# Two heads of the first tile moved from the expert phase into the front of a decoder-step kernel

## The chip, the cores and the metric

The kernel runs on one core of one Trainium2 chip. The metric is the device time of one execution in microseconds (us), the median of several runs. The profile is of one further execution, with its own time.

## What is computed

One layer of a hybrid decoder on 1024 prompt tokens and 32 sample tokens (8 sequences of 4), all in float32, width 1024. The part that matters here:

```python
h = h + concat(pooling_mixer, conv_module) @ w_out
# PEER product-key experts on x = rmsnorm(h) * g_ffn, blocks of 128 tokens
q = (x @ w_q).reshape(tokens, 8, 2, 128)            # 8 heads, 2 halves
s = einsum('thpc,hpkc->thpk', q, sub_keys)          # 128 keys for each half
sv, si = top_k(s, 16)
cand = sv[:, :, 0, :, None] + sv[:, :, 1, None, :]  # 256 candidates
top_s, top_j = top_k(cand, 16)
eidx = take(si0 * 128 + si1, top_j); gate = softmax(top_s)
u, v = u_tab[eidx], v_tab[eidx]                     # 16384 x 1024 each
coef = gate * gelu(sum(x * u)); h = h + sum(coef * v)
```

Before it stands an input projection with the two mixers, behind it a gated embedding and a final norm. For every token and head 16 rows of 4 KB are gathered from u_tab and 16 from v_tab.

## The kernel before

The kernel is one program with an instruction stream written out for each engine. It has two phases, `front` and `experts`. A phase ends for all engines together: an engine enters the second when all have ended the first.

`front` treats the first four prompt tiles (512 tokens) and the 32 samples: norm, input projection, mixers, layer norm of the convolution, and the output projection. Its last loop goes over two spans of columns (`th` 0: 256 tokens, `th` 1: 288) and eight pieces of the output (`n`). PE makes one product of four matmuls into one of four PSUM results (line 590; the same result is used again four products later, behind `added`). DVE adds it to `hT` (line 733) and adds the squares of the product before to `total` (line 724). ACT squares the piece (line 419) and writes it times the gain `g_ffn` into `xg_a` (lines 422, 424), the input of the queries. SP loads the two first pieces of `w_q` (`wq`, a ring of two, 1 MB each) in the front already; POOL has nothing to do at its end.

`experts` goes over 66 blocks: 64 of one prompt tile and one head (128 tokens by 16 picks), and two of samples. Queries and scores are made in units: the units 0 and 1 (`ALONE`) are heads 0 and 1 for tile 0 alone, the next ones are half a head for the tiles together. `query(s)` (line 1373) and `scores(s)` (line 1384) are PE's, ACT copies the query and scales the scores by `rstd` (lines 1102, 1112), and DVE makes `pick(s)` (lines 1687 to 1697, the best 16 of 128 in two rounds of 8) and `rank_tile` (lines 1703 to 1726, the best 16 of 256, their table indices `eidx` and the shifted scores). POOL issues a gather for each pick (line 1066), one of u and one of v by turns, v 20 picks behind u. The u rows go to a ring of 8, the v rows to a ring of 7. DVE makes the dot product of a u row with the normed tokens `xn` (line 1772), ACT a diagonal matrix of the coefficients (line 1188), and PE multiplies it by the v row and sums in `acc` (line 1671). Later blocks also hold the mixers of the other four tiles, step by step, and the embedding.

At the start of `experts`, SP first issues the broadcast of `g_ffn`, two tiles of x, and then the next pieces of `wq`, each when a query unit has freed its place. PE makes query 0, the means of squares for four tiles, scores 0, query 1, scores 1, turns tile 0, then units 2 to 5. DVE picks and ranks head 0, then head 1, makes `xn`, and begins with the dots. POOL's first gather waits for the first rank (`ranked`).

Of the kernel before, what the change touches and what calls it, by code (L numbers as in the profile page):

```python
# [128 lines left out]
AHEAD_OF_NORM = 5  # L129
WQ_RING = 2  # L130
# [7 lines left out]
def front(nc, io, M):  # L138

    with Phase(nc, "fr") as ph:  # L140
# [33 lines left out]
        part = xT  # L174
        recent = bass.AP(tensor=ufull_s[:, :, :].tensor, offset=0, ap=((DEC_B * (CONV_PRE + DEC_S), P), (CONV_PRE + DEC_S, DEC_B), (1, DEC_S), (1, TAPS)))
# [14 lines left out]
        keys_turned, keys_out = ph.sem("keys_turned"), ph.sem("keys_out")  # L190
# [24 lines left out]
        def gate_count(c):  # L215

            return c + 2

        @block.sync
        def _(sp):  # L220
# [89 lines left out]
        def _(act):  # L310
# [74 lines left out]
            for r in range(4):  # L385
                act.wait_ge(keys_turned, r + 1)
                nc.scalar.copy(flat(M.keysT[:, 4 * r:4 * r + 4, :]), extra[:, r % 2, :]).then_inc(keys_out, 1)
# [24 lines left out]
            nc.scalar.activation(std[:, n_all + 1:n_all + 2], M.eps[:, :], ACT.Sqrt)  # L412
            for th, cols in enumerate(SPANS):
                for n in range(DC):
                    act.wait_ge(added, DC * th + n + 1)
# [3 lines left out]
                    nc.scalar.activation(osq[n % 2][:, cols], M.hT[:, n, cols], ACT.Square).then_inc(squared, 1)  # L419
                    gain = M.vec[:, VEC["g_ffn"] + n:VEC["g_ffn"] + n + 1]  # L420
                    stop = min(cols.stop, SA)
                    nc.scalar.activation(M.xg_a[:, n, cols.start:stop], M.hT[:, n, cols.start:stop], ACT.Copy, scale=gain)
# [4 lines left out]
        def _(pe):  # L427
# [89 lines left out]
            for r in range(4):  # L517
                pe.wait_ge(keys_in, 32)
                if r >= 2:

                    pe.wait_ge(keys_out, r - 1)
                for k in range(4):
                    last = nc.tensor.transpose(extra[:, r % 2, k * P:(k + 1) * P], keys[:, 4 * r + k, :], M.ident[:, :])
                last.then_inc(keys_turned, 1)
# [10 lines left out]
            pe.wait_ge(keys_out, 4)  # L535
# [39 lines left out]
            for n in range(AHEAD_OF_NORM + 1, DC):  # L575
                pool_half(n)
            for th, cols in enumerate(SPANS):
                for n in range(DC):
                    if n == 0:
# [14 lines left out]
        def _(dve):  # L594
# [130 lines left out]

            for th, cols in enumerate(SPANS):
                for n in range(DC):
                    m = DC * th + n
                    if th == 0 and n + 2 in range(AHEAD_OF_NORM, DC):
                        add_part(n + 2)  # L730
                    dve.wait_ge(part_added, n + 1)
                    dve.wait_ge(projected, m + 1)
# [15 lines left out]
HEAD_FIRST = 2  # L748
# [113 lines left out]
def experts(nc, io, M):  # L862

    with Phase(nc, "ex") as ph:
# [11 lines left out]
        eidx = [ph.sb(f"eidx{b}", [P, TOPK], U32) for b in range(KEPT)]  # L876
# [1230 lines left out]
```

## Time and profile before

| | |
|---|---|
| median of 3 runs | 3347.69 us (3325.36 to 3354.73) |
| the profiled execution's own time | 3370.43 us |
| its span, first to last instruction | 3368.6 us |
| mean granted TensorE clock | 0.931 of full |
| PE / DVE / ACT / POOL busy | 80% / 67% / 24% / 62% |
| bytes moved by DMA | 1167.87 MB, 347 GB/s over the span |

Busy shares are means over stages that differ. The rows below give start times in us from the span's start. In a timeline row the second number is the time from the group's start to its end, xN the number of instructions, and the bracket the idle time before it with what ended that.

### The profile page before, as it was taken

How to read it: one execution, taken by the hardware profiler on the slowest of the kernel's cores; microseconds unless marked ns; L12 is line 12 of the kernel's file. 1: busy time of each engine (PE TensorE's matmuls, PEld its weight loads, DVE VectorE, ACT ScalarE, POOL GpSimd, SP SyncE). 2: the span in 40 equal slices, each digit the busy share in tenths (PEclk: the TensorE clock that was granted, in tenths of full speed). 3: DMA queues.
4: the chain of work that ended last, by engine and by line, in shares of the span. 5: the costliest groups of instructions: out<-in, count | busy, mean ns of one | idle time of the engine just before them, and what ended most of it. 6: DMA issues, size and time to landing. Idle time of an engine off the chain costs nothing.

```text
span 3368.6 us, 24895 instructions
## 1 busy us (share of the span) xinstructions
PE 2698.3 (80%) x6723; PEld 1222.9 (36%) x6723; DVE 2268.0 (67%) x5244; ACT 815.5 (24%) x1946; POOL 2097.5 (62%) x2169
## 2 busy tenths in 40 slices
PE   8989888888978767677688887789878888678867
PEld 7754433333333323333344442233323333223322
DVE  8867668897875766767767565656566668555545
ACT  2332322223131211111112222222222222112212
POOL 2135666676766667566566666666666667666664
PEclk9999998999999988888899989999999999899998
DMA  5269999999999999899899999999999999999996
GB/s 142 70 236 354 359 367 346 381 387 377 377 363 350 396 368 370 331 354 346 326 367 373 360 361 410 386 367 376 378 365 365 376 376 371 357 360 367 374 370 211
DMA packets 363167, 1167.87 MB, mean 347 GB/s; under 512 B 35401, under 2 KB 88217, under 8 KB 363029
## 3 DMA queue, kind: packets, MB, share of 16 engines
q0 software_dynamic: 304128, 1107.43, 86.5%
q1 hardware_dynamic: 58368, 58.02, 5.3%
q8 instruction: 57, 0.93, 0.1%
q10 hardware_dynamic: 533, 0.83, 0.1%
q14 instruction: 81, 0.66, 0.1%
HBM read 1160.98 MB, written 5.15 MB: 346 GB/s over the span
## 4 chain that ended last, share of the span: by engine, by line
PE 22%; DVE 19%; POOL 15%; issue 13%; another core or an unknown queue 13%; DMA 10%; ACT 2%; DVEq 0%; POOLq 0%; ACTq 0%
PE ex_acc L1671 14%; DVE ex_u_row L1772 8%; POOL ex_v_row L1066 8%; POOL ex_u_row L1066 7%; DMA ex_u_row<-in_u_tab_dram,ex_eidx 5%; DMA ex_v_row<-in_v_tab_dram,ex_eidx 4%; PE ex_q L1373 3%; PE ex_turn L1429 2%; DVE m_mix L1865 1%; PE ex_q L1429 1%; DVE m_hT L1790 1%; DVE ex_lists L1697 1%; DVE ex_lists L1690 1%; DVE ex_same L1691 1%
## 5 line engine op out<-in xcount | busy, mean ns | idle before, releaser
L1671 PE MATMUL ex_acc<-ex_v_row,ex_diag 128*128 128x512 f32 x3840 | 1919.3, 639 | 556.3 <-DMA ex_v_row<-in_v_tab_dram,ex_eidx 290.5
L1772 DVE CUSTOM_DVE_ANT_0 ex_u_row<-ex_u_row,ex_xn 128x1024 f32<-128x1024 f32 x1056 | 1256.2, 1217 | 482.0 <-DMA ex_u_row<-in_u_tab_dram,ex_eidx 358.8
L1066 POOL DMA_INDIRECT ex_v_row<-in_v_tab_dram,ex_eidx x1024 | 995.2, 972 | 598.1 <-issue 271.8
L1671 PEld LDWEIGHTS ex_acc<-ex_v_row,ex_diag 128*128 128x128 f32 x3840 | 726.7, 201 | 1651.8 <-issue 1503.5
L1066 POOL DMA_INDIRECT ex_u_row<-in_u_tab_dram,ex_eidx x1024 | 996.0, 973 | 527.4 <-issue 285.2
L1188 ACT ACTIVATE ex_diag<-m_ident,ex_coef 128x128 f32<-128x128 f32 x948 | 318.7, 393 | 737.4 <-issue 326.6
L1373 PE MATMUL ex_q<-m_mix,m_wq 128*128 128x384 f32 (+3 forms) x832 | 238.4, 441 | 2.4 <-PEq L95 1.9
L1373 PEld LDWEIGHTS ex_q<-m_mix,m_wq 128*128 128x128 f32 x832 | 143.1, 193 | 104.0 <-issue 66.9
L1102 ACT COPY ex_qT<-ex_q 128x384 f32<-128x384 f32 (+3 forms) x50 | 22.0, 440 | 475.5 <-remote 313.4
L1384 PE MATMUL ex_s<-m_keysT,ex_qT 128*128 128x128 f32 x288 | 54.1, 328 | 79.3 <-ACT ex_qT L1102 63.4
L1790 DVE SCALAR_TENSOR_TENSOR m_hT<-ex_v_row,ex_coef,m_hT 128x1024 f32<-128x1024 f32 x76 | 97.4, 1282 | 0.0
L1763 DVE SCALAR_TENSOR_TENSOR ex_coef<-ex_expo,ex_norm,ex_hact 128x16 f32<-128x16 f32 x64 | 15.2, 238 | 117.9 <-issue 70.6
L1510 PE MATMUL ex_turn<-m_hT,m_wq 128*128 128x512 f32 x192 | 89.0, 607 | 5.4 <-ACT m_mix L1214 5.4
L1772 DVE DVE_READ_ACCUMULATOR2_ANT ex_hdot<- 128x1 f32 x1056 | 87.7, 83 | 0.4 <-issue 0.4
L1384 PEld LDWEIGHTS ex_s<-m_keysT,ex_qT 128*128 128x128 f32 x288 | 44.8, 219 | 111.5 <-ACT ex_qT L1102 75.7
L1112 ACT ACTIVATE ex_score<-ex_s,ex_rstd 128x128 f32<-128x128 f32 (+1 forms) x144 | 42.3, 363 | 174.1 <-PE ex_s L1384 87.0
L1277 ACT ACT_TABLE_LOAD x65 | 83.4, 1283 | 1.1
L1865 DVE SCALAR_TENSOR_TENSOR m_mix<-m_mix,m_taps 128x512 f32<-128x512 f32 x109 | 82.3, 755 | 1.3 <-issue 0.9
L1118 ACT ACT_TABLE_LOAD x63 | 80.8, 1283 | 1.1
L1694 DVE MAX8 ex_lists<-ex_same 128x8 f32<-128x128 f32 (+1 forms) x144 | 32.6, 281 | 63.1 <-remote 60.5
L1277 ACT ACTIVATE ex_hact<-ex_hdot 128x16 f32<-128x16 f32 x66 | 14.2, 215 | 233.5 <-DVE ex_hdot L1772 159.2
L1429 PE MATMUL ex_turn<-m_mix,m_wq 128*128 128x512 f32 x128 | 61.3, 624 | 6.2 <-ACT m_wq L1142 6.2
(371 smaller groups left out, 2037.6 us busy)
## 6 DMA issues: line engine op xcount, KB each, us to landing
m_wq<-in_w_q_dram SPq DMA_DIRECT2D x18, 1024.0 KB
ex_u_row<-in_u_tab_dram,ex_eidx POOLq DMA_INDIRECT x1024
ex_v_row<-in_v_tab_dram,ex_eidx POOLq DMA_INDIRECT x1024
fr_w<-in_w_in_dram SPq DMA_DIRECT2D x12, 512.0 KB, 4.3
m_wq<-in_w_in_dram SPq DMA_DIRECT2D x6, 1024.0 KB
m_wq<-in_w_out_dram SPq DMA_DIRECT2D x4, 1024.0 KB
m_mix<-in_w_ple_gate_dram SPq DMA_DIRECT2D x8, 512.0 KB
out_y_prompt_dram<-m_wq SPq DMA_DIRECT2D x7, 512.0 KB
```

Of the source, the lines that this page charges most:

```text
L1066: pool.indirect_dma_start(out=row[:, :], out_offset=None, in_=table, in_offset=bass.IndirectOffsetOnAxis(ap=picks(b)[:, k:k + 1], axis=0)) ...
L1118: nc.scalar.activation(expo[r % KEPT][:, :], shift[r % 2][:, :], ACT.Exp, accum_out=norm[r % KEPT][:, :]).then_inc(exped, 1)
L1188: nc.scalar.activation(diag[:, n % DIAGS, 0:rows(t)], pattern[:, :], ACT.Copy, scale=coef[b % 2][:, k:k + 1]).then_inc(diaged, 1)
L1277: nc.scalar.activation(hact[b % 2][:, :], hdot[b % 2][:, :], ACT.Gelu_apprx_tanh).then_inc(gelued, 1)
L1373: last = nc.tensor.matmul(q_ps[:, out:out + cols], weights(load, c), xg[:, c, at:at + cols], start=(c == 0), stop=(c == DC - 1))
L1384: last = nc.tensor.matmul(s_ps[0:rows(t), j * P:(j + 1) * P], qT[:, s % 2, j * P:j * P + rows(t)], keysT[:, half, :], start=True, stop=True)
L1429: last = nc.tensor.matmul(gate_out[:, :], x2T[:, c, :], w_gate[:, c, cols], start=(c == 0), stop=(c == DC - 1))
L1510: last = nc.tensor.matmul(late_bank[n % 2], weights(late_load(n), c), late_h[:, c, :], start=(c == 0), stop=(c == DC - 1))
L1671: last = nc.tensor.matmul(acc[0:rows(t), half, :], diag[:, tensor_sums(n) % DIAGS, 0:rows(t)], row[:, half * HALF_D:(half + 1) * HALF_D], ...
L1772: nc.vector.tensor_tensor_reduce(out=u_row[n % U_RING][:, :], in0=u_row[n % U_RING][:, :], in1=xn[:, :], scale=1.0, scalar=0.0, op0=ALU.mu ...
L1790: ins = nc.vector.scalar_tensor_tensor(out=tokens, in0=row[:, :].rearrange("p (c e) -> p c e", c=DC), scalar=coef[b % 2][:, k:k + 1], in1= ...
L1865: nc.vector.scalar_tensor_tensor(out=u, in0=src, scalar=tap[:, j:j + 1], in1=u, op0=ALU.mult, op1=ALU.add).then_inc(late_tapped, 1)
```

## The change

The units 0 and 1 leave `experts`. Their work is done in the last loop of `front`, in its second span. PE makes one mean (tile 0) and query 0 ahead of product 1, scores 0 ahead of product 2, query 1 ahead of product 3, scores 1 ahead of product 4. ACT takes the root, the two query copies and the two scaled scores between its squares. DVE makes the reciprocal ahead of add 1, pick 0 ahead of add 2, the rank of head 0 ahead of add 3 and pick 1 ahead of add 5. The query and score use columns of `val` and `gate` that no result uses, and the small tiles lie in `xin`, which is free by then. In the first span ACT now writes the gained tokens ahead of the square. The lists of head 1, the index list and the shifted scores of head 0 get tiles that outlive the front. SP loads the next two pieces of `wq` in the front too, each behind the query that frees its place.

At the start of `experts` the semaphores are counted up for what is done already, DVE begins with the rank of head 1, and PE begins with the four means (now into `s_ps`), turns tile 0 and goes on with unit 2. The reciprocals of the four tiles come behind the rank.

```diff
+HEAD_FIRST = 2
+QUERY_BEFORE = (1, 3)
+SCORE_BEFORE = (2, 4)
...
# front, SP
+            for n in range(WQ_RING):
+                sp.wait_ge(projected, query_count(n))
+                sp.dma_start(M.wq[:, n], wq_cols[:, :, 2 * (n + WQ_RING) * P:2 * (n + WQ_RING + 1) * P]).then_inc(M.wq_in[n], 16)
...
# front, ACT
+            def first_root():
+                act.wait_ge(meaned, len(SPANS) + 1)
+                nc.scalar.activation(first_std, small[:, 0, 0:1], ACT.Sqrt, bias=M.eps[:, 0:1]).then_inc(rooted, 1)
+
+            def first_query_out(h):
+                act.wait_ge(projected, query_count(h))
+                if h > 0:
+
+                    act.wait_ge(keyed, 4 + h)
+                nc.scalar.copy(flat(first_qT), first_q).then_inc(part_out, 1)
+
+            def first_scores_out(h):
+                act.wait_ge(keyed, 4 + h + 1)
+                act.wait_ge(inverted, n_all + 1)
+                nc.scalar.activation(flat(first_score[h]), first_s, ACT.Copy, scale=first_rstd).then_inc(keyed_out, 1)
+
             for th, cols in enumerate(SPANS):
                 for n in range(DC):
+                    if th == 1 and n == 1:
+                        first_root()
+                        first_query_out(0)
+                    if th == 1 and n == 2:
+                        first_scores_out(0)
+                    if th == 1 and n == 3:
+                        first_query_out(1)
+                    if th == 1 and n == 4:
+                        first_scores_out(1)
...
# front, PE
+            def first_mean():
+                pe.wait_ge(totalled, DC + 1)
+                pe.wait_ge(added, DC)
+                nc.tensor.matmul(small[:, 0, 0:1], M.total[:, 0:P], M.mean_d[:, 0:1], start=True, stop=True).then_inc(meaned, 1)
+
+            def first_query(h):
+                pe.wait_ge(squared, n_all + 2 * MC + DC)
+                pe.wait_ge(M.wq_in[h], 16)
...
+                for half in range(2):
+                    for c in range(DC):
+                        last = nc.tensor.matmul(first_q[:, half * P:(half + 1) * P], M.wq[:, h, c, half * P:(half + 1) * P], M.xg_a[:, c, 0:P],
+                                                start=(c == 0), stop=(c == DC - 1))
+                last.then_inc(projected, 1)
...
# front, DVE: first_pick(h) and first_rank_head() have the steps of pick and rank_tile
                     m = DC * th + n
+                    if th == 1 and n == 1:
+                        dve.wait_ge(rooted, n_all + len(SPANS) + 1)
+                        nc.vector.reciprocal(first_rstd, first_std).then_inc(inverted, 1)
+                    if th == 1 and n == 2:
+                        first_pick(0)
+                    if th == 1 and n == 3:
+                        first_rank_head()
+                    if th == 1 and n == 5:
+                        first_pick(1)
...
# experts, SP
-            for pair in range(WQ_RING, LOADS // 2):
+            for pair in range(2 * WQ_RING, LOADS // 2):
...
# experts, PE
-            query(0)
+            pe.sem_inc(q_done, ALONE)
+            pe.sem_inc(scored, ALONE)
             for t in range(A_TILES):
-                last = nc.tensor.matmul(turn[:, 0, t:t + 1], M.total[:, t * P:(t + 1) * P], M.mean_d[:, 0:1], start=True, stop=True)
+                last = nc.tensor.matmul(s_ps[:, t:t + 1], M.total[:, t * P:(t + 1) * P], M.mean_d[:, 0:1], start=True, stop=True)
             last.then_inc(meaned, 1)
-            scores(0)
-            query(1)
-            scores(1)
-            pe.wait_ge(rooted, 1)
             turn_tokens(0)
-            for s in range(2, EARLY):
+            for s in range(ALONE, EARLY):
                 query(s)
+                if s == ALONE:
+                    pe.wait_ge(rooted, 1)
                 scores(s)
...
# experts, DVE
+            dve.sem_inc(picked, ALONE)
+            dve.sem_inc(ranked, 1)
+            dve.sem_inc(shifted, 1)
+            rank_tile(1)
             dve.wait_ge(rooted, 1)
             nc.vector.reciprocal(rstd[:, 0:A_TILES], std[:, 0:A_TILES]).then_inc(inverted, 1)
-            for head in range(HEAD_FIRST):
-                pick(head)
-                dve.wait_ge(picked, head + 1)
-                rank_tile(head)
+            dve.wait_ge(inverted, 1)
```

## Rows read from the trace of the kernel before

**Rows 1.** The page, DMA queues: packets, MB, share of 16 engines

```profile
q0 software_dynamic: 304128, 1107.43, 86.5%
...
q14 instruction: 81, 0.66, 0.1%
```

**Rows 2.** Windows by stage: length, busy time by engine, clock, DMA share, GB/s

```profile
207.50:300.00 92.50, 74.54 (x207) 35.74 (x206) 70.30 (x221) 24.02 (x61) 56.32 (x59) 0.90 0.94 349
300.00:1000.00 700.00, 598.37 (x1393) 260.53 (x1392) 557.16 (x1325) 189.06 (x479) 465.73 (x471) 0.94 0.97 371
1000.00:2000.00 1000.00, 765.07 (x1888) 352.04 (x1888) 676.90 (x1715) 198.30 (x510) 644.28 (x660) 0.90 0.95 357
2000.00:3000.00 1000.00, 792.72 (x1751) 317.90 (x1750) 608.18 (x1311) 254.60 (x563) 667.50 (x696) 0.95 0.98 374
3000.00:3330.00 330.00, 247.83 (x540) 94.16 (x539) 170.74 (x306) 69.30 (x156) 217.40 (x223) 0.93 0.95 357
```

**Rows 3.** Timeline of PE, 150 to 214 us

```profile
175.25 2.10 PE L590 MATMUL fr_val<-fr_mix,fr_wout 128*128 128x288 f32 x8
...
188.84 2.10 PE L590 MATMUL fr_small<-fr_mix,fr_w 128*128 128x288 f32 x8
192.88 3.81 PE L1373 MATMUL ex_q<-m_mix,m_wq 128*128 128x128 f32 x32 [1.94 <-PEq L95]
196.53 0.95 PE L1606 MATMUL ex_turn<-m_mean_d,m_total 128*128 128x1 f32 x8
197.34 0.69 PE L1384 MATMUL ex_s<-m_keysT,ex_qT 128*128 128x128 f32 x4
...
204.07 7.11 PE L1373 MATMUL ex_q<-m_mix,m_wq 128*128 128x512 f32 x16 [0.42 <-DMA m_wq<-in_w_q_dram]
```

**Rows 4.** Timeline of DVE, 150 to 214 us, then 213 to 262 us

```profile
185.23 0.46 DVE L733 TENSOR_TENSOR m_hT<-m_hT,fr_val 128x288 f32<-128x288 f32 x1 [1.12 <-PE fr_val L590]
185.60 0.45 DVE L724 TENSOR_TENSOR m_total<-m_total,fr_odd 128x288 f32<-128x288 f32 x1
...
192.01 0.46 DVE L724 TENSOR_TENSOR m_total<-m_total,fr_odd 128x288 f32<-128x288 f32 x1
...
198.84 0.49 DVE L1687 MAX8 ex_lists<-ex_score 128x8 f32<-128x128 f32 x2 [0.86 <-ACT ex_score L1112]
...
201.71 0.43 DVE L1703 TENSOR_TENSOR ex_cand<-ex_lists 128x256 f32<-128x256 f32 x1
...
207.01 0.17 DVE L1721 SCALAR_TENSOR_TENSOR ex_eidx<-ex_idx 128x16 uint32<-128x16 f32 x1
...
215.52 1.29 DVE L1960 SCALAR_TENSOR_TENSOR ex_xn<-m_hT,ex_rstd,ex_g_ffn 128x1024 f32<-128x1024 f32 x1
```

**Rows 5.** Timeline of ACT, 150 to 214 us

```profile
192.28 0.30 ACT L424 ACTIVATE m_mix<-m_hT,m_vec 128x32 f32<-128x32 f32 x1
```

**Rows 6.** Timeline of POOL, 180 to 420 us

```profile
207.47 1.15 POOL L1066 DMA_INDIRECT ex_u_row<-in_u_tab_dram,ex_eidx  x1 [85.18 <-DVE ex_eidx L1721]
```

**Rows 7.** Timeline of SP, 100 to 330 us

```profile
192.85 0.38 SPq L1024 DMA_DIRECT2D ex_g_ffn<-in_g_ffn_dram  x1
193.27 0.89 SPq L1022 DMA_DIRECT2D ex_lists<-in_x_prompt_dram  x2
```

**Rows 8.** Windows of 2 to 5 us, columns as in rows 2

```profile
206.00:208.00 2.00, 2.00 (x6) 0.81 (x5) 1.90 (x9) 0.31 (x2) 0.53 (x1) 1.00 0.12 38
208.00:210.00 2.00, 2.00 (x6) 0.95 (x5) 1.93 (x13) 0.00 (x0) 1.56 (x2) 1.00 0.27 39
210.00:212.00 2.00, 1.32 (x4) 0.35 (x3) 1.86 (x8) 0.58 (x1) 1.52 (x2) 1.00 0.93 324
...
260.00:265.00 5.00, 5.00 (x19) 2.79 (x18) 4.76 (x15) 0.13 (x2) 3.75 (x4) 1.00 0.60 186
```

**Rows 9.** Waits of ACT, then of DVE, whole span: us in total, times, longest

```profile
ACT ex_qT L1102 <- remote: 313.4, 22, 21.9
...
DVE ex_lists L1694 <- remote: 60.5, 11, 8.0
```

More of the change, by code:

```diff
@@ L217, in gate_count, with output_count, query_count @@
             return c + 2
+        def output_count(th, n):
+            return DC * th + n + 1 + (sum(n >= QUERY_BEFORE[h] for h in range(HEAD_FIRST)) if th == 1 else 0)
+        def query_count(h):
+            return output_count(1, QUERY_BEFORE[h]) - 1
         @block.sync
@@ L385, in _ @@
             for r in range(4):
-                act.wait_ge(keys_turned, r + 1)
-                nc.scalar.copy(flat(M.keysT[:, 4 * r:4 * r + 4, :]), extra[:, r % 2, :]).then_inc(keys_out, 1)
+                act.wait_ge(keyed, r + 1)
+                nc.scalar.copy(flat(M.keysT[:, 4 * r:4 * r + 4, :]), extra[:, r % 2, :]).then_inc(keyed_out, 1)
             for g in range(MC):
@@ L576, in _, with first_scores @@
                 pool_half(n)
+            def first_mean():
[5 more added lines that the diff above has]
+                pe.wait_ge(M.wq_in[h], 16)
+                if h > 0:
+                    pe.wait_ge(part_out, DC + h)
+                for half in range(2):
[3 more added lines that the diff above has]
+                last.then_inc(projected, 1)
+            def first_scores(h):
+                pe.wait_ge(part_out, DC + h + 1)
+                if h > 0:
+                    pe.wait_ge(keyed_out, 4 + h)
+                for half in range(2):
+                    last = nc.tensor.matmul(first_s[:, half * P:(half + 1) * P], first_qT[:, half, :], M.keysT[:, 2 * h + half, :],
+                                            start=True, stop=True)
+                last.then_inc(keyed, 1)
             for th, cols in enumerate(SPANS):
                 for n in range(DC):
+                    if th == 1 and n == QUERY_BEFORE[0]:
+                        first_mean()
+                        first_query(0)
+                    if th == 1 and n == SCORE_BEFORE[0]:
+                        first_scores(0)
+                    if th == 1 and n == QUERY_BEFORE[1]:
+                        first_query(1)
+                    if th == 1 and n == SCORE_BEFORE[1]:
+                        first_scores(1)
                     if n == 0:
@@ L724, in total_squares, with first_pick @@
                 nc.vector.tensor_tensor(M.total[:, cols], M.total[:, cols], osq[m % 2][:, cols], ALU.add).then_inc(totalled, 1)
+            def first_pick(h):
+                values, at = head_lists[h][:, 0], head_lists[h][:, 1].bitcast(U32)
+                dve.wait_ge(keyed_out, 4 + h + 1)
+                for half in range(2):
+                    last = nc.vector.max(values[:, half, 0:8], first_score[h][:, half, :])
+                chain.step(last)
+                for half in range(2):
+                    nc.vector.max_index(at[:, half, 0:8], values[:, half, 0:8], first_score[h][:, half, :])
+                    last = nc.vector.match_replace(first_rest[:, half, :], values[:, half, 0:8], first_score[h][:, half, :], NEG)
+                chain.step(last)
+                for half in range(2):
+                    last = nc.vector.max(values[:, half, 8:16], first_rest[:, half, :])
+                chain.step(last)
+                for half in range(2):
+                    last = nc.vector.max_index(at[:, half, 8:16], values[:, half, 8:16], first_rest[:, half, :])
+                chain.step(last)
@@ L1343, in _ @@
             few_sigmoids(2)
-            nc.scalar.activation(few_moment[:, 3:4], M.eps[0:TS, 0:1], ACT.Sqrt)
+            nc.scalar.activation(few_moment[:, 2:3], M.eps[0:TS, 0:1], ACT.Sqrt)
             act.wait_ge(few_biased, 1)
```

77 lines of the change are left out of this document (59 added, 18 removed).

## The prediction

> **What bounds the kernel now.** I read the queues first. Gathers from the two expert tables (POOL's software queue) are 1107 MB of the kernel's 1168 MB and alone fill 86.5% of the sixteen DMA engines' span [rows 1]. Then the windows by stage: from 300 to 3330 us the DMA engines are 95 to 98% busy at 357 to 374 GB/s, while PE is busy 75 to 85% of the time, DVE 52 to 80% and POOL about two thirds [rows 2]. So behind the first gathers the time is bytes through the DMA engines. 2112 gathers of 0.524 MB have to pass, and an edit that leaves these bytes alone can only change when the stream begins, how full it is kept, and the tail. The reader is to see that DMA share is the one column near 1 in every long stage. The change touches the 192.6 to 300 us stretch and nothing behind it, where the share is already 0.94 [rows 2].
>
> Then the order of work at the seam. PE's last output product starts at 188.84 us [rows 3], DVE's last sum of squares is at 192.01 [rows 4], ACT's last gain ends at 192.58 [rows 5], and 0.3 us later PE has its first instruction of the experts' phase, at 192.88 [rows 3]. POOL's first gather comes at 207.47 [rows 6], right behind the write of the first index list at 207.01 [rows 4]. These 14.9 us between seam and first gather are what the change goes for.
>
> **Part 1, PE in the front.** One query of 32 matmuls takes from 192.88 to 196.53, 3.65 us; four mean matmuls take 0.81, so one is 0.2; the four score matmuls take 0.69 alone, 0.55 with the overlap at their end [rows 3]. Output products of the second span start 1.94 us apart: (188.84 - 175.25) / 7 [rows 3]. The mean added ahead of product 1 needs the sum of square 7, which DVE does only behind the add of product 0: for the product that starts at 183.01 (four steps behind 175.25) that pair ends at 186.05, 3.0 us after the product's start [rows 3, 4]. So the mean can start at 178.3 while product 0 ends at 177.2: a new wait of 1.1 us on PE; behind it on PE are all the other products. PE's front grows by 1.1 + 0.2 + 2 x 3.65 + 2 x 0.55 = 9.7 us, and its last product ends near 200.5.
>
> **Part 2, DVE in the front.** A pick takes from 198.84 to 201.71, 2.9 us; the ranking from 201.71 to 207.18 (the index list's 207.01 + 0.17), 5.5 us [rows 4]; the added reciprocal of one column I take at 0.2, like the shortest DVE row there. Together 2 x 2.9 + 5.5 + 0.2 = 11.5 us. An add and a sum of squares take 0.82 us of the 1.94 us step [rows 4], so DVE has 1.1 us free in each step, far less than it gets. Followed through: the first query ends at 182.2, product 1 at 184.1, the first scores at 184.7; ACT turns to them behind its own square and gains, and the first pick starts near 186.0. Three pieces (2.9 + 5.5 + 2.9), six add and sum pairs (4.9) and the last sum (0.45) then run nearly without a gap, to 202.7; with waits for ACT's squares between them I take 203.9, and ACT's last gain 204.1. Queued behind the picks are the adds of products 2, 3 and 5, for which ACT's squares wait. PE wants a bank back only four products later, and by this count never stands for an add: product 7 wants the add of 3, done at 195.9, and starts at 198.5. DVE, then, not PE, ends the front: 204.1 against 192.6, 11.5 us later. Bounds: 202.7 (no waits) and 206.5 (a further 1.1 us wait for each of ACT's two score copies).
>
> **Part 3, the first gather.** The index list is there when the phase opens, so POOL needs the 0.3 us of the seam and 0.3 us as between 207.18 and 207.47 [rows 4, 6]: 204.1 + 0.6 = 204.7 or 204.8. That is 2.7 us earlier than now; bounds 203.3 and 207.1, so 4.2 to 0.4 us earlier. 14.9 us are taken out behind the seam, 11.5 put in ahead of it, and that is why the large move pays little.
>
> **Part 4, the other queues.** SP issues the two weight pieces (1 MB each) behind query 0 and query 1 in the front, near 182 and 190, where nothing else moves. They landed before 207 so far, ahead of the first gather, in time the DMA engines would mostly have stood: the share is 0.12 in 206 to 208 and 0.27 in 208 to 210 [rows 8]. So moving them out frees almost nothing; they saved only the 0.42 us wait of PE at 204.07 [rows 3]. What was not moved matters more: the gain vector's broadcast and two x tiles, 0.5 MB each, go out when the phase opens, at 192.85 and 193.27 [rows 7]. Now they were through long before the gathers; after the change they are issued in the same microsecond as the first gather. 1.5 MB at 371 GB/s (the mean of the 300 to 1000 window [rows 2]) is 4.0 us. Some 2.3 us of that fits into the time in which the first row is being set up (gather at 207.47, full rate only from 210 [rows 6, 8]), so rows arrive 0 to 4.0 us later than their issue would allow; I take 1.7. Net of part 3: 1.0 us earlier, between 4.2 earlier and 3.6 later.
>
> By the Trainium skill ("DMA: Bandwidth & Descriptors", section "Queues, rings and completion order") each DMA engine takes turns between the queue rows that have work, packet by packet. By that rule the three loads would halve the first rows' rate rather than hold them all back; the bytes, and so the sum, stay the same.
>
> **Part 5, DVE and PE in the new phase.** DVE starts with the second ranking (5.5), then xn (1.3), so its first dot comes near 211.6; now it follows xn at 215.52 + 1.3 = 216.8 [rows 4]: 5 us earlier. But dots then wait for rows, which are 1 us ahead. PE's units 2 to 5 come later: query 2 starts behind the means and the turn of tile 0 at 206.4, against 204.07 [rows 3]. Their scores are first picked behind sixteen dots, whose rows come no faster than 0.524 MB / 371 GB/s = 1.41 us each, so not before 211.6 + 16 x 1.41 = 234; units 2 and 3, 7.1 us each [rows 3] and some 1.5 for copy and scores, end near 223.6. That cover of 10 us makes the cost nothing; without it it is 2.3 us. A last piece is a hole in the DMA stream: 0.60 busy from 260 to 265 [rows 8], 2 us lost there, when DVE was late with picks and dots. With DVE 5 us ahead it may shrink by these 2 us or stay: I take half, 1 us earlier.
>
> **Sum.** 1.0 + 1.0 = 2 us earlier. On the profiled execution 3370.4 - 2 = 3368.4. Its span is 3368.6 and the rest of it is 1.8. The median of the runs shown is 22.7 us below it, and the gain is not a share of the length, so 3347.7 - 2 = 3345.7.
>
> **Rivals.** (a) The head start counts in full: the loads hide wholly in the set-up time, DVE's 5 us fill both the hole at 260 and the ones behind it. For it: POOL waits on DVE's dots in that stretch. Against it: a ring of eight rows, which DVE empties faster than they come. It gives 4.2 + 5 = 9 us less, 3338.5. (b) Slower, by stalls of the engines in straight code. ACT waits 313.4 us in 22 times ahead of its query copies for something that the profile calls remote, up to 21.9 us, and DVE does so between two steps of one pick, up to 8.0 us [rows 9]. The instruction queue moves its own packets on the same DMA engines [rows 1]. A saturated stream now begins earlier, with loads on top. If one more such wait of 21.9 falls on ACT ahead of the first gate or diagonal, the rings' fifteen rows cover 15 x 0.524 MB / 371 GB/s = 21 us less what already waits; with half of them in hand, 11 us are lost: 3347.7 - 2 + 11 = 3356.7. It decides if the first weighted sum starts over 10 us later against the first gather than now. The Trainium skill ("Runtime: NRT & Kernel Launch", section "Instruction fetch mechanics") says that the fetch across a block is mostly hidden; by that rule this rival would cost nothing, but it has no account of the remote waits seen here. (c) The change doesn't start the gathers earlier: DVE's front stretches to 206.5 or more, the loads then delay the rows by up to 4: 3347.7 + 3.6 = 3351.
>
> **How the numbers follow.** Chances: forecast 0.5, (a) 0.17, (b) 0.15, (c) 0.13, and 0.05 for something that no row shows. All four lie within 11 us, a third of 1%. The three runs before lie from 3325.4 to 3354.7, so 1% (33 us) is about what a measurement can tell, and this spread, not the mechanism, makes the range: 3320 (the lowest run less 5) to 3361 (the highest and half of (b)). Faster by over 1%: 0.06, from (a) with a lucky spread and a part of the unknown; slower by over 1%: 0.06, from (b) twice; within 1%: 0.88.
>
> **What would show it.** The phase opens near 204, the first gather is near 204.8, the first dot near 211.6; DVE has no gap over 1 us between the first front pick and the last sum; PE's products keep their 1.94 us step except at the queries; the DMA share from 300 on stays 0.95 to 0.98. I am wrong if PE waits for adds, if the front ends behind 206.5, or if the time moves by more than 10 us, which would need the DMA's rate in the long stages to have changed.

## The result, and the profile after

The changed kernel takes 3354.15 us (median of 21 runs, 3345.12 to 3379.32) against 3346.15 us (21 runs, 3313.93 to 3364.1) on the same chip: ratio 1.0042, 95% interval 1.0023 to 1.006. That is 8 us slower by the medians and 14 us by the ratio. The profiled execution took 3359.54 us with a span of 3357.7; it is shorter than the profiled one of before (3368.6), so the ends of two single profiles can't show the loss. The gathers, in order, show where the stream falls behind:

```
start of POOL's n-th gather, us      n=0    n=8    n=20   n=28   n=32   n=48   n=60   n=100  n=200  n=300
before                              207.5  219.2  235.1  250.4  260.2  285.2  302.2  367.0  524.6  670.8
after                               203.9  215.3  230.2  247.3  266.5  289.2  313.5  377.6  534.1  680.8
after minus before                   -3.5   -3.9   -5.0   -3.1   +6.2   +4.0  +11.3  +10.6   +9.5   +9.9
```

The stream starts 3.5 us early, keeps that for 28 gathers, and is 10 us late from the 60th on. Behind the 400th the difference wanders between 10.5 us early and 14.1 us late; the last gather starts 10.2 us earlier than before. So these two profiles show the lag at the start, and not what is left of it at the end.

The seam first: the changed kernel's timelines of PE, DVE, ACT, SP and POOL, columns as in [rows 3 to 7].

```profile
197.43 2.10 PE L684 MATMUL fr_small<-fr_mix,fr_w 128*128 128x288 f32 x8
203.48 1.02 PE L1747 MATMUL ex_s<-m_mean_d,m_total 128*128 128x1 f32 x8 [3.95 <-PEq L95]
...
205.57 8.42 PE L1513 MATMUL ex_q<-m_mix,m_wq 128*128 128x512 f32 x16
```

```profile
202.31 0.46 DVE L818 TENSOR_TENSOR m_total<-m_total,fr_odd 128x288 f32<-128x288 f32 x1 [0.48 <-ACT fr_odd L478]
...
211.53 1.22 DVE L1913 CUSTOM_DVE_ANT_0 ex_u_row<-ex_u_row,ex_xn 128x1024 f32<-128x1024 f32 x1 [1.11 <-DMA ex_u_row<-in_u_tab_dram,m_first_idx]
```

```profile
202.58 0.31 ACT L482 ACTIVATE m_mix<-m_hT,m_vec 128x32 f32<-128x32 f32 x1
```

```profile
203.15 0.35 SPq L1165 DMA_DIRECT2D ex_g_ffn<-in_g_ffn_dram  x1
203.55 0.90 SPq L1163 DMA_DIRECT2D ex_lists<-in_x_prompt_dram  x2
```

```profile
203.94 1.15 POOL L1207 DMA_INDIRECT ex_u_row<-in_u_tab_dram,m_first_idx  x1 [82.54 <-DVEq L2088]
...
266.47 0.94 POOL L1207 DMA_INDIRECT ex_u_row<-in_u_tab_dram,ex_eidx  x1 [14.47 <-DVE ex_hdot L1913]
```

The front ends at 202.9, 10.3 us later than before (192.58 [rows 5]), and the first gather comes 3.5 us earlier. But the last line is a gather that waited 14.47 us for a free row. The windows show what that did to the stream (columns as in [rows 8], the long ones as in [rows 2]).

```profile
206.00:208.00 2.00, 2.00 (x3) 0.68 (x2) 1.89 (x5) 1.98 (x2) 1.70 (x2) 0.50 0.99 338
208.00:210.00 2.00, 2.00 (x6) 0.91 (x5) 1.91 (x5) 0.44 (x3) 1.39 (x3) 0.91 1.01 412
...
255.00:260.00 5.00, 4.37 (x16) 2.52 (x17) 0.39 (x3) 3.34 (x8) 0.00 (x0) 1.00 0.84 266
260.00:265.00 5.00, 5.00 (x13) 2.28 (x12) 4.86 (x33) 2.04 (x6) 0.00 (x0) 1.00 0.02 8
265.00:270.00 5.00, 5.00 (x19) 2.63 (x18) 4.86 (x13) 0.26 (x1) 2.81 (x3) 1.00 0.34 98
...
207.50:300.00 92.50, 67.95 (x189) 32.95 (x189) 63.77 (x188) 17.53 (x50) 48.16 (x51) 0.89 0.88 328
300.00:1000.00 700.00, 601.78 (x1404) 259.19 (x1404) 555.34 (x1326) 199.41 (x494) 466.75 (x472) 0.95 0.98 371
1000.00:2000.00 1000.00, 760.77 (x1896) 349.88 (x1895) 678.40 (x1717) 195.12 (x503) 646.88 (x663) 0.90 0.95 358
2000.00:3000.00 1000.00, 795.26 (x1752) 322.03 (x1751) 605.43 (x1303) 254.06 (x563) 662.48 (x695) 0.95 0.98 375
```

From 206 to 210 the DMA engines are full where they stood at 0.12 and 0.27 [rows 8]. From 260 to 265, where they were 0.60 busy, they now stand still: 8 GB/s. The stretch to 300 falls from 0.94 to 0.88; the long stages are as before [rows 2].

Why POOL waits is read backwards. POOL's rows come free with DVE's dots. DVE's timeline shows what stood ahead of them: the coefficients of block 0, which waited for ACT's Gelu. ACT's timeline shows why the Gelu was late, after first and then before:

```profile
259.62 0.23 DVE L1904 SCALAR_TENSOR_TENSOR ex_coef<-ex_expo,ex_norm,ex_hact 128x16 f32<-128x16 f32 x1 [11.34 <-ACT ex_hact L1417]
```

```profile
236.86 1.14 ACT L1253 ACTIVATE ex_score<-ex_s,ex_rstd 128x128 f32<-128x128 f32 x4 [12.78 <-remote]
...
244.04 0.59 ACT L1243 COPY ex_qT<-ex_q 128x512 f32<-128x512 f32 x1 [5.85 <-remote]
246.79 1.14 ACT L1253 ACTIVATE ex_score<-ex_s,ex_rstd 128x128 f32<-128x128 f32 x4 [2.16 <-PE ex_s L1524]
255.00 0.59 ACT L1243 COPY ex_qT<-ex_q 128x512 f32<-128x512 f32 x1 [7.06 <-PE ex_q L1513]
256.83 1.14 ACT L1253 ACTIVATE ex_score<-ex_s,ex_rstd 128x128 f32<-128x128 f32 x4 [1.25 <-PE ex_s L1524]
...
259.29 0.21 ACT L1417 ACTIVATE ex_hact<-ex_hdot 128x16 f32<-128x16 f32 x1
```

```profile
237.08 1.14 ACT L1112 ACTIVATE ex_score<-ex_s,ex_rstd 128x128 f32<-128x128 f32 x4 [7.88 <-remote]
247.86 0.58 ACT L1102 COPY ex_qT<-ex_q 128x512 f32<-128x512 f32 x1 [9.63 <-remote]
250.61 1.14 ACT L1112 ACTIVATE ex_score<-ex_s,ex_rstd 128x128 f32<-128x128 f32 x4 [2.17 <-PE ex_s L1384]
...
253.06 0.22 ACT L1277 ACTIVATE ex_hact<-ex_hdot 128x16 f32<-128x16 f32 x1
```

In both kernels ACT stands in a wait that the profile calls remote until about 237. Before, it held the scores of unit 4, and only unit 5 was left; after, it held the scores of unit 3, and units 4 and 5 were left. PE had begun its units 1.5 us later and run the first query slower (8.42 us instead of 7.11 [rows 3], at a granted clock of 0.50 in 206 to 208). But the wait is also there earlier: PE ended unit 3's scores at 225.3 and ACT did not take them, while before ACT still copied unit 4's query at 228.61. The experiments tell how far PE's delay counts. ACT's order puts the units 4 and 5 ahead of block 0's Gelu in both kernels. The Gelu slips from 253.06 to 259.29, though its last dot ended at 234, not 239. DVE waits 11.34 us for it with the next dots queued behind. The gather that comes at 266.47 waits for one of these dots.

### The profile page after: what moved, and what is told of

The parts are those of the page before. It is cut to its first block, busy times and chain, and to the rows that moved or that the text cites. A ratio compares the mean times of both kernels' runs of the same rounds, so it can differ in the third digit from the quotient of the medians.

```text
span 3357.7 us, 24911 instructions
## 1 busy us (share of the span) xinstructions
PE 2688.2 (80%) x6725; PEld 1217.1 (36%) x6725; DVE 2268.1 (68%) x5245; ACT 815.4 (24%) x1945; POOL 2090.1 (62%) x2169
## 4 chain that ended last, share of the span: by engine, by line
DVE 20%; PE 18%; POOL 17%; issue 14%; another core or an unknown queue 12%; DMA 11%; ACT 2%; DVEq 0%; POOLq 0%; ACTq 0%
PE ex_acc L1810 12%; POOL ex_u_row L1207 8%; POOL ex_v_row L1207 8%; DVE ex_u_row L1913 8%; DMA ex_v_row<-in_v_tab_dram,ex_eidx 5%; DMA ex_u_row<-in_u_tab_dram,ex_eidx 4%; PE ex_q L1513 3%; DVE m_mix L2006 1%; DVE m_hT L1931 1%; DMA ex_u_row<-in_u_tab_dram,m_first_idx 1%; PE ex_turn L1569 1%; PE ex_q L1569 1%; ACT ex_diag L1329 1%; DVE ex_same L1855 1%
## 5 line engine op out<-in xcount | busy, mean ns | idle before, releaser
L1207 POOL DMA_INDIRECT ex_v_row<-in_v_tab_dram,ex_eidx x768 | 741.8, 966 | 455.4 <-issue 200.6
L1207 POOL DMA_INDIRECT ex_u_row<-in_u_tab_dram,ex_eidx x768 | 745.3, 970 | 348.8 <-issue 217.9
L1207 POOL DMA_INDIRECT ex_u_row<-in_u_tab_dram,m_first_idx x256 | 249.7, 976 | 185.3 <-DVEq L2088 82.5
L1207 POOL DMA_INDIRECT ex_v_row<-in_v_tab_dram,m_first_idx x256 | 250.1, 977 | 143.2 <-issue 69.4
L1513 PE MATMUL ex_q<-m_mix,m_wq 128*128 128x384 f32 (+2 forms) x768 | 231.6, 455 | 0.0
L1513 PEld LDWEIGHTS ex_q<-m_mix,m_wq 128*128 128x128 f32 x768 | 135.9, 194 | 101.4 <-issue 64.3
L1243 ACT COPY ex_qT<-ex_q 128x384 f32<-128x384 f32 (+2 forms) x48 | 21.3, 443 | 407.9 <-remote 253.4
```

The lines of the kernel that those rows point to most:

```text
L1207: pool.indirect_dma_start(out=row[:, :], out_offset=None, in_=table, in_offset=bass.IndirectOffsetOnAxis(ap=picks(b)[:, k:k + 1], axis=0)) ...
L1513: last = nc.tensor.matmul(q_ps[:, out:out + cols], weights(load, c), xg[:, c, at:at + cols], start=(c == 0), stop=(c == DC - 1))
```

## The experiments

The order of work in block 0 after the change, on ACT: copy and scores of units 2, 3, 4, 5, then the Gelu, then the diagonals. Theory G says that the Gelu's place behind the units costs the hole. The rivals are the loads beside the first gathers, PE's later start, and its clock. The expectations name more theories by letters: Q is the earlier and wider form of G (the coefficients of block 0 are queued on ACT and PE behind late units), L the loads beside the first gathers, R a cost in the later stages, N a mere scatter of the runs, D the depth of the queued gathers as the reason of ACT's waits. All ratios are to the kernel before on the same chip. Gathers are compared with those of the first profile of before, unless said otherwise; a second profile of that same kernel has gather 0 1.7, gather 32 4.6 and gather 100 1.2 us earlier.

**The loads.** The two x tiles are issued behind the next pair of weight pieces (near 224) instead of in the opening:

```diff
-            load_x(0)
-            load_x(1)
             for pair in range(2 * WQ_RING, LOADS // 2):
                 ...
+                if pair == 2 * WQ_RING:
+                    load_x(0)
+                    load_x(1)
```

> The changed kernel, with the loads of the two x tiles (1 MB) issued behind the next weight piece, near 224, and no longer beside the first gathers. Theory L: rows come up to 2.7 us earlier at the start, the hole near 260 shrinks, ratio 1.001 or less. Theory Q: the rows of the first dots come earlier but the Gelu still waits for unit 5; the ratio stays within 0.1% of 1.004.

Ratio 1.0035 (1.0003 to 1.0068). The first dot comes at 211.22 with no wait for its row, but DVE waits 11.9 us for the Gelu, gather 32 is 6.8 and gather 100 13.1 us later than before. The loads are not the cause.

**PE later in the kernel before.** Sixteen products of the identity ahead of unit 2:

```diff
+            pe.wait_ge(q_out, 2)
+            for j in range(16):
+                nc.tensor.matmul(q_ps[...], M.ident[:, :], M.ident[:, :], start=True, stop=True)
             for s in range(2, EARLY):
```

> The kernel before with 16 added products of the identity (128 columns, some 3.7 us) on PE ahead of unit 2, their result unused: nothing of the front, the gathers' start or the loads changes, only PE's units come later. Theory Q: this alone brings the changed kernel's picture, one unit fewer done when ACT's long wait comes, DVE waiting about 10 us for the first Gelu and a hole in the DMA stream; ratio 1.002 to 1.005. Theories L and R, and a delay that is hidden: 0.999 to 1.001.

Ratio 1.0026 (1.0001 to 1.0052). Unit 2's query starts at 207.21, 3.1 us later than before, twice the delay that the change brings. ACT's unexplained waits hold unit 4's copy to 240.46 (14.31 us), the Gelu comes at 255.97 (before: 253.06), DVE waits 5.1 us (10 were expected), gather 32 is 2.9 and gather 100 8.2 us late. Twice the delay of PE gives half of the lag at gather 32: a delay of PE alone can do damage, but doesn't account for all of it.

**PE kept running at the seam.** The same sixteen products at the end of the changed kernel's front, so that PE does not idle 3.95 us ahead of the phase:

> The changed kernel with 16 products of the identity (3.7 us, unused) on PE at the end of the front, where it stood idle from 199.5 to 203.5 and its granted clock then fell to half in 206 to 208. If idle PE and its clock make the units late: query 2 takes 7.1 us instead of 8.4, unit 3 is ready 1.4 us earlier, gather 100 comes 1 to 5 us earlier, ratio 1.001 to 1.004. If not: gather 100 at 376 to 379 and the ratio within 0.1% of 1.004; above 1.005 if the added products themselves delay the phase.

```profile
204.66 7.03 PE L1516 MATMUL ex_q<-m_mix,m_wq 128*128 128x512 f32 x16
```

The first query is back at 7.03 us and starts a microsecond earlier (PE's timeline), 0.6 us later than before. The hole stays: an unexplained wait of 18.43 us on ACT ends at 243.51, the Gelu comes at 259.1, DVE waits 11.6 us, gather 32 is 6.0 us late; ratio 1.0064 (1.0032 to 1.0097). Gather 100 is 8.0 us late and not 10.6, which is within the gain that the expectation asked for; two profiles of the kernel before differ by 1.2 us at that gather and by 4.6 at gather 32, so 2.6 us may be scatter. So the clock does not make the hole, nor does PE's late start have to: with PE only 0.6 us late the hole is whole. Which of ACT's steps the wait hits decides, and why it hits an earlier one in the changed kernel, where the gathers start earlier too, was not tested.

**The Gelu ahead of unit 5 on ACT.**

```diff
+                if s == 4:
+                    act.wait_ge(dotted, TOPK)
+                    nc.scalar.activation(hact[0][:, :], hdot[0][:, :], ACT.Gelu_apprx_tanh).then_inc(gelued, 1)
```

> The changed kernel; only on ACT the Gelu of block 0 moves ahead of unit 5's query and scores, PE's order stays. If the queue on ACT alone makes the loss: DVE's wait for the Gelu falls from 11.3 us to under 3, gather 32 at 256 instead of 266.5, gather 100 at 367 to 370, ratio 1.000 to 1.002. If PE's lateness makes it (units 5 and 6 stand ahead of the first weighted sum on PE, which starts at 263.5): gather 32 comes earlier but POOL then waits for a v row to be summed, gather 100 stays at 375 to 378, ratio 1.003 to 1.005.

ACT's timeline and two windows of this kernel:

```profile
242.61 1.14 ACT L1253 ACTIVATE ex_score<-ex_s,ex_rstd 128x128 f32<-128x128 f32 x4 [16.95 <-remote]
...
250.14 0.21 ACT L1417 ACTIVATE ex_hact<-ex_hdot 128x16 f32<-128x16 f32 x1
255.59 0.58 ACT L1243 COPY ex_qT<-ex_q 128x512 f32<-128x512 f32 x1 [5.24 <-PE ex_q L1517]
```

```profile
260.00:265.00 5.00, 5.00 (x13) 2.13 (x12) 4.79 (x13) 0.70 (x2) 0.74 (x1) 1.00 0.95 341
...
207.50:300.00 92.50, 74.20 (x208) 36.29 (x206) 64.52 (x189) 21.58 (x55) 53.63 (x57) 0.92 0.96 360
```

The unexplained wait is there, longer than in the changed kernel (16.95 us against 12.78), and PE is as late (unit 5's copy at 255.59, first weighted sum at 264.10). Still the hole at 260 to 265 is gone (0.95 against 0.02), gather 32 comes at 257.3, 2.9 us ahead of before, and gather 100 is 2.1 us late instead of 10.6. Only the Gelu's place was changed: that order is what lets the wait through to the stream. Ratio 1.0004 (0.9965 to 1.0043), where the kernel with the added products took 1.0064 on the same chip. A second series:

> The same kernel as a_gelu_first, for a narrower interval: 1.0004 with 0.9965 to 1.0043 did not part it from the changed kernel's 1.0042. If ACT's queue ahead of block 0's Gelu makes the loss (theory G): 0.999 to 1.002 again, gather 32 near 257, gather 100 near 369. If the first value was luck: 1.003 to 1.006.

1.0017 (0.9992 to 1.0042), gather 32 4.3 us early, gather 100 5.5 us late. Ahead of unit 4 instead (`if s == 3`):

> The changed kernel with the Gelu of block 0 one unit earlier still, behind unit 3's scores and ahead of unit 4's query on ACT. It waits for the sixteenth dot (near 235), so unit 4's query copy and PE's query 5 come about 10 us later. Theory G alone: as a_gelu_first or up to 2 us better, 0.998 to 1.002. If PE's units now become the bound as they did in two_later: gather 32 near 255, gather 100 at 372 or later, ratio over 1.003.

The Gelu ran at 240.37; 1.0011 (0.9977 to 1.0044), gather 32 5.6 us early, gather 100 5.5 us late, as above. What is left is a smaller loss behind gather 32, where POOL waits for PE's weighted sums (15.7 us in 257 to 310, in the first of the three).

**The same place tried on the kernel before.** The Gelu ahead of unit 5:

> The kernel before with the Gelu of block 0 ahead of unit 5's query and scores on ACT. There DVE waited only 2.0 us for it, so theory G gives a gain of 2 us at most: ratio 0.998 to 1.000, gather 32 at 257 to 260, gather 100 at 363 to 367. A kernel-wide effect of the moved Gelu (table loads, order) that has nothing to do with the wait would give this kernel the same 0.4% that it gives the changed one: 0.996.

0.9981 (0.9954 to 1.0008): gather 32 2.3 us early, gather 100 4.9 us early, but the interval holds 1. And the reverse, the Gelu held until unit 6's query is done (`act.wait_ge(q_done, EARLY + 1)` ahead of it):

> The kernel before with one added wait: ACT makes the Gelu of block 0 only when the query of unit 6 is done on PE (258.9 in the trace of before), as if one more unit stood ahead of it. Nothing else is touched, and the gathers start at 207.5. Theory G: DVE waits 7 to 9 us for the Gelu instead of 2.0, POOL waits for the dots behind it, the DMA share falls under 0.4 somewhere in 255 to 270, gather 100 at 372 to 377, ratio 1.002 to 1.004. If a hole there is made up for later: 1.000.

Waits of DVE and windows of this kernel:

```profile
DVE ex_coef L1765 <- ACT ex_hact L1279: 10.6, 1, 10.6
```

```profile
260.00:265.00 5.00, 4.75 (x11) 2.20 (x12) 4.86 (x32) 1.84 (x6) 0.00 (x0) 1.00 0.00 0
```

With nothing of the change in it, one late Gelu (259.19) makes the same hole, and gather 32 is 6.1 us late as in the changed kernel (6.2), gather 100 6.4 late and not the 10 that the changed kernel is. The ratio, 1.0022 (0.9993 to 1.0052), has an interval that holds 1.

**Fewer units ahead of block 0.** Units 4 and 5 moved into block 0's sums, four units there instead of two, in the changed kernel and in the one before:

```diff
-EARLY = 6
+EARLY = 4
...
+                    if b == 0 and k in (0, 5, 10, 13):
+                        query(EARLY + (0, 5, 10, 13).index(k))
```

> The changed kernel, but only units 2 and 3 are made ahead of block 0; units 4 and 5 move into it (units 4 to 7 at its picks 0, 5, 10 and 13), so ACT meets the Gelu of block 0 behind unit 3's scores. Theory Q (the coefficients of block 0 are queued on ACT and PE behind units 2 to 5, and the change makes these units late): ACT's Gelu comes within 3 us of the sixteenth dot (near 240, not 259.3), DVE's wait of 11.3 us ahead of the first coefficients and the hole in the DMA stream near 260 go, gather 60 comes at 303 or earlier instead of 313.5, and the time is 0.2 to 0.6% under the changed kernel's, so 0.998 to 1.002 of the kernel before. Theory L (what costs is the broadcast and the two x tiles beside the first gathers): nothing of that changes, the ratio stays at 1.004. Theory R (the later stages pay, through other tile places or other timing of waits): 1.004 too, with gather 60 early all the same.

> The kernel before with the same order of units. Theory Q: there the Gelu stood at 251.8 behind unit 5 and DVE waited 2.0 us for it, PE's first weighted sum came at 258.7; with the units later both come near 245 to 250, the dip of the DMA share at 260 to 265 shrinks, and the ratio is 0.996 to 1.000. With a_two_later it then gives what the early gather alone is worth: 3 to 4 us. Theories L and R: 1.000, and a_two_later minus this stays at +0.4%.

1.008 (1.0052 to 1.0108) and 1.0081 (1.005 to 1.0111). The hole goes (gather 32 is 5.7 and 4.7 us early), but PE can't carry two more units in block 0: in the first, PE is busy throughout 290 to 340 and the DMA engines are at 0.67.

```profile
290.00:340.00 50.00, 48.56 (x137) 23.34 (x136) 20.29 (x68) 14.71 (x35) 18.57 (x20) 1.00 0.67 224
```

Gather 100 is 19.6 and 18.1 us late. That both kernels lose the same, with first gathers 3.9 us apart, speaks for it that an early first gather is worth nothing where PE sets the pace. Spreading the units over the blocks instead (EARLY = 4, two per block up to block 6, two late products moved with them; units 16 and 17 then read a part of the input that the late mixer has already overwritten, so these two compute other picks there):

> The changed kernel, with units 2 and 3 alone ahead of block 0 and two units in each of the blocks 0 to 6 (before: four ahead and two in each of 0 to 5); one pair of late weights is scaled, and its product made, a few picks later in block 6. What two_later showed: the hole at 250 to 266 goes (gather 32 at 254.6, not 266.5), but four units of 8 us in block 0 put PE behind. Theory Q': early PE work and its order are the bound of the first blocks; with two units in each block PE never has more than 2 x 8 + 16 x 1.7 = 43 us of work in a block whose rows take 32 x 1.41 = 45 us, so the lead of 4 to 6 us at gather 32 stays: gather 100 at 361 to 368 against 367.0 before and 377.6 changed, ratio 0.996 to 1.000. Rival: PE has fallen behind for good in any order, since the same units have to be made before block 6; gather 100 then comes at 375 or later, ratio 1.003 to 1.008.

> The kernel before with the same units in the same blocks. Theory Q': gather 32 near 256 (now 260.2), gather 100 at 363 to 369, ratio 0.998 to 1.001, and 0.001 above a_spread, by the 3.5 us that the gathers start later. Rival: as for a_spread, 1.003 to 1.008.

1.004 (1.0007 to 1.0073) and 1.0019 (0.999 to 1.0048). The start is good (gather 100 is 4.0 us early in the first), and it is lost between gathers 220 and 260, where PE makes the last two of these units: from 6.3 us early to 10.4 late in the first, from 1.9 early to 12.6 late in the second.

**A chip without these waits.** The next four kernels ran on another chip:

> The changed kernel itself, once more, timed beside the two reordered ones so that they can be compared directly. Theory G (the Gelu of block 0 stands in ScalarE's order behind unit 5's copy and scores, VectorE's coefficients wait 11 us for it, and the transfers have a hole at 260 to 265): a ratio of 1.003 to 1.006 to the kernel before, VectorE's wait for the Gelu 10 to 12 us, gather 32 about 6 us and gather 100 about 10 us later than before. Rival N (the first result was a scatter of the runs, as the single profiles scatter by 10 us and more): a ratio of 1.000 to 1.002.

> The changed kernel with block 0's Gelu ahead of unit 5's query copy on ScalarE, beside the changed kernel in the same series. Theory G: 0.002 to 0.004 below the ratio of the changed kernel, that is 1.001 to 1.002, with VectorE's wait for the Gelu 1 to 3 us, gather 32 at 3 to 4 us earlier than before and gather 100 at 2 to 5 us later. Rival N: the same ratio as the changed kernel to 0.001.

> The kernel before with the same reordering on ScalarE, the version that could beat both; its first series gave 0.9981 with an interval that holds 1. Theory G gives it 2 us (the wait of VectorE for the Gelu is 2.0 us before, and gather 32 came 2.3 us earlier): 0.9994, hardly to be told from 1. If the first series is to be taken at its word, 0.998.

> The changed kernel where GpSimd keeps only four gathered rows ahead of the dots during the first 32 gathers, so that fewer transfers stand in the queues at 210 to 240 us. If ScalarE's long unexplained wait (12.78 us, ending at 236.86) comes from the depth of the queued gathers (theory D), it shrinks to under 5 us, the Gelu starts before 255 and VectorE's wait for it is under 5 us; the time is then 1.000 to 1.003. If the depth has nothing to do with it, the wait stays at 8 to 15 us, ends at 237 or later, and the hole stays; the time is 1.004 or more, since the gathers come later too.

The kernel before takes 3077.06 us there, the changed one 3077.3 (ratio 1.0000, 0.9991 to 1.0009), the Gelu ahead of unit 5 3076.92 in the changed kernel (1.0001, 0.9992 to 1.001) and 3076.97 in the one before (0.9998, 0.9989 to 1.0008). Windows and ACT's timeline of the changed kernel there:

```profile
260.00:265.00 5.00, 5.00 (x13) 2.28 (x12) 5.00 (x9) 0.00 (x0) 3.74 (x4) 1.00 0.98 339
...
300.00:1000.00 700.00, 623.44 (x1489) 269.73 (x1488) 581.86 (x1346) 205.87 (x510) 511.68 (x509) 0.98 1.02 402
```

```profile
232.08 0.59 ACT L1243 COPY ex_qT<-ex_q 128x512 f32<-128x512 f32 x1 [5.53 <-PE ex_q L1513]
...
245.07 0.21 ACT L1417 ACTIVATE ex_hact<-ex_hdot 128x16 f32<-128x16 f32 x1
```

No engine shows a remote wait in the whole span. PE is as late at the start as in the first profile (its query takes 8.01 us), yet the Gelu runs at 245.07, DVE waits 3.5 us for it, and the share stays at 0.98. So the hole needs the unexplained wait as well as the order. The loads beside the gathers, the late PE and its clock are all there, and no hole. The first gather at 204.6 and the full queues hold a lead of 2.7 us at the start and 1.7 at gather 300 over the kernel before with its Gelu moved (a profile of the kernel before itself wasn't taken on this chip); at the end it is 1.9 us behind. A gain of 2 us is within what this series can't see.

The kernel with four rows in flight tells nothing on why ACT waits, as no wait was there to shrink; but it prices a hole. POOL waited 28.7 us for dots up to 270 us; it was 20.9 us behind the changed kernel at gather 28, 11.2 at gather 100, 12.4 at gather 300 and 12.7 at the last, and took 3092.66 us, 15.4 more (to the kernel before 1.0055, 1.0039 to 1.007). Between gathers 28 and 60 it gained 9 us back, for there the changed kernel's own stream stood for dots. From then on nothing was regained: what the stream is behind at gather 60 (11.8 us), it is behind at the end.

**Both once more, side by side.**

> The kernel before itself, as a profile beside the changed one on the same chip. The last series ran on a chip whose profiles hold none of ScalarE's long unexplained waits and move 402 to 406 GB/s from 300 us on (371, 358 and 375 in the first profiles); there all kernels but the one with four rows took 3077 us. On such a chip theory G expects: no unexplained wait, the Gelu of block 0 within 3 us of its last dot and unit 5, gather 100 at 351 to 353 us (the reordered one: 351.2), and the ratio of the kernel to itself 1.000. On a chip as in the first series: 3340 to 3370 us, an unexplained wait of ScalarE of 7 to 15 us that ends at 237 to 248, VectorE's wait for the Gelu 2 to 4 us, gather 100 at 364 to 370 us.

> The changed kernel beside it. Theory G: on a chip without the unexplained waits a ratio of 0.999 to 1.001 and gather 100 at 349 to 350 us, 2 us earlier than the kernel before, with a transfer share above 0.9 at 250 to 270; on a chip with them 1.003 to 1.006, VectorE's wait for the Gelu 8 to 12 us, a share under 0.4 somewhere at 255 to 270, gather 100 5 to 12 us later than the kernel before. Rival N (a scatter): no difference on either.

This was a chip of the first kind. The first gathers are at 205.81 and 203.34, so the head start is 2.5 us here. The windows at 260 us, the kernel before first:

```profile
260.00:265.00 5.00, 5.00 (x13) 2.14 (x12) 4.90 (x10) 0.00 (x0) 1.63 (x3) 1.00 0.78 292
```

```profile
260.00:265.00 5.00, 5.00 (x13) 2.28 (x12) 4.90 (x28) 1.17 (x3) 0.00 (x0) 1.00 0.01 2
```

The hole is back, with 13.44 us of unexplained wait on unit 3's scores to 236.87, 11.1 us of DVE for the Gelu, and gather 100 at 379.3 against 365.8. But the times are 3345.66 for the changed kernel and 3344.24 for the kernel before. Each was set against the same 23 further runs of the kernel before (3341.66): 1.0007 (0.9977 to 1.0037) for the changed one, and 1.0006 (0.9976 to 1.0036) for that kernel against itself. The loss of the first series is not seen here, though the hole is; the two intervals share 1.0023 to 1.0037. The spans of the two profiles of one and the same kernel before are 3368.6 and 3318.0 us.

## Why the prediction was wrong

It said 2 us faster; it was slower, by 8 us of the medians and 14 by the ratio. That the time lies inside the range given comes from the spread of the runs, which made the range, and not from the mechanism.

**Parts 1 to 3 held**, within a microsecond or so. PE's last product starts at 197.43 and ends at 199.5 (said: 200.5), with a wait of 0.95 us for the mean (said 1.1). DVE's last sum of squares is at 202.31, ACT's last gain ends at 202.9 (said 204.1, bounds 202.7 to 206.5): DVE ended the front, and it stood less for ACT's squares than I allowed. The first gather came 3.5 us earlier, and 2.5 in the second pair of profiles (said 2.7).

**Part 4 held in its sign.** DVE had `xn` ready at 210.42 and waited 1.11 us for the first row, to 211.53; I had allowed 1.7 us for the loads. Moved away, they freed this wait and changed nothing behind it. That 211.53 is so near to the 211.6 of part 5 is luck: that was DVE's own work, counted from a gather at 204.8, without a wait for the row.

**Part 5 failed**, at one sentence: PE's units 2 to 5 come later, and a "cover of 10 us makes the cost nothing". I measured the cover at the place where DVE picks from the units. There it held: DVE picked from unit 2 at 234.02 without a wait, as said (234). But ACT, which has to copy them, is a queue too, and block 0's Gelu stands behind them. Nothing in the sum asked what was queued behind ACT's copies, and my row on the remote waits [rows 9] stood only in a rival. The cover ended at the Gelu: its last dot was ready at 234, it ran at 259.29. That a reordering of this one step takes the hole away with PE as late as ever, and that one late Gelu puts it into the kernel before, is shown. The dip at 260 to 265, which I let shrink by 1 us, deepened: the DMA share there fell from 0.60 to 0.02.

**Rival (b)** was nearest: a stall of ACT in straight code, 3356.7 us. Its waits were the ones that mattered, but they need not be more or longer than before (ACT's copies wait 253.4 us for "remote" in 21 times, 313.4 in 22 before [rows 9]), and its point of decision, the first weighted sum over 10 us later against the first gather, came to 8.3: 263.50 - 203.94 = 59.6 against 258.74 - 207.47 = 51.3. The place was the Gelu, not the first diagonal. Rival (c)'s 3351 us is as near to the measured time, but its condition failed: the front ended at 202.9, not at 206.5 or later. In the changed kernel's trace no packet of the instruction queues starts between 215.4 and 249.0 us, a stretch that holds both waits of ACT, to 236.86 and to 244.04. So these waits don't test the rule of the Trainium skill ("Runtime: NRT & Kernel Launch", section "Instruction fetch mechanics") that instruction fetch is mostly hidden.

**Whether 10 us are regained** depends on the slack behind them. On the faster chip, with a share of 1.02, they are not: the kernel with four rows was 11.8 us behind at gather 60 and 12.7 at the end. On the first chips the share is 0.95 to 0.98, which leaves 2 to 5% of 3000 us, over 60 us, in which a lag could be made up. No run shows whether it is, so the step from the hole to the 8 to 14 us of the first series is argued, not shown.

**What stays open.** What the remote waits are, and why they hit ACT earlier in the changed kernel. In 14 of the 16 profiles on the first chips one of ACT's ends between 241 and 248, whichever step stands there (the other two, kernels before with fewer units ahead, have none of over 1.5 us there); earlier ones end anywhere from 225 to 240. And how much of the 10 us at gather 100 reaches the end on such a chip: the kernels with the hole gave 1.0042 and 1.0007 (the change), 1.0035, 1.0064, 1.0026 and 1.0022; the changed kernel with the Gelu moved 1.0004, 1.0017 and 1.0011. On the whole the order fits, but the changed kernel's own second value (1.0007) lies among those without the hole, and the single intervals overlap. No version was shown to beat the kernel before; with the Gelu ahead of unit 5 it gave 0.9981 and 0.9998, both intervals holding 1.

## What to carry to other kernels

When a step comes later, look for cover on every in-order queue that it passes through, not at its last reader: here the copies' reader had 10 us, and the Gelu queued behind the copies had none. Put the step on which a ring's release depends ahead of work that is needed later. In a kernel bound by a stream, an earlier start is worth only what the stream keeps: here a head start of 3.5 us was gone in one hole by the 32nd gather, and on the chip without the hole a head start of 2.7 us could not be seen in the time.

## What the runs showed of the hardware

The kernel before took 3341 to 3368 us on some chips and 3077 on another. The changed kernel, with the same bytes, moved 402 GB/s at a share of 1.02 there against 371 at 0.98 in 300 to 1000 us. The difference goes with the remote waits: ACT, DVE and POOL stand in 762, 238 and 172 us of them in the profile of before, in none on the faster chip, where the DMA engines are busier. So a full DMA stream alone does not bring them about, as rival (b) had it. Whether the waits slow the stream, or both have one cause, is not shown.

After 3.95 us without work PE was granted 0.50 of its clock in 206 to 208 (1.2 GHz), and its query took 8.42 us; with sixteen more products in the gap it was granted 1.00 there, and the query took 7.03. On the other chip the query behind the same gap took 8.01.
